# Differential attention: context units apart, and which engine scales which map

## The reference, cut to what matters

```python
def diff_attend(q, k, v, lam):
    s = jnp.einsum('bqhcd,bkhcd->bhcqk', q, k) * (q.shape[-1] ** -0.5)
    p = jax.nn.softmax(s.astype(jnp.float32), axis=-1)
    a = (p[:, :, 0] - lam * p[:, :, 1]).astype(v.dtype)
    return jnp.einsum('bhqk,bkhd->bqhd', a, v)
```

## Time and profile before

| what | value |
|---|---|
| median of 3 runs | 4229.64 us (4227.66 to 4230.34) |
| profiled execution | 4231.93 us, span 4230.1 us, clock 0.984 |
| busy, share of span | PE 94%, PE weight load 64%, DVE 40%, ACT 24%, POOL 19% |
| stage in layer 0 | from about 1886 to 1980 us of the span |
| stage in layer 1 | from about 3358 to 3431 us of the span |

### The profile page before, as it was taken

One profiled execution on the slowest core, in us unless ns is written; L12 is line 12 of the kernel. 1 busy time (PEld: TensorE's weight loads), 2 busy tenths in 40 slices (PEclk: granted clock), 3 DMA queues, 4 the chain that ended last, 5 costly groups with the idle time before them and its releaser, 6 DMA issues. The chain is left out here.

```text
span 4230.1 us, 65478 instructions
## 1 busy us (share of the span) xinstructions
PE 3996.5 (94%) x28448; PEld 2713.6 (64%) x28448; DVE 1671.5 (40%) x2600; ACT 1035.7 (24%) x2175; POOL 812.5 (19%) x640
## 2 busy tenths in 40 slices
PE   8999999999999999998999799999899999979888
PEld 6788889887888767566555443333576778833332
DVE  2585854374444342627434300000436464421102
ACT  2212521222111221516211321111314252221111
POOL 2100022113442021113233101000131234400000
PEclk9999999999999999999999899999999999989999
DMA  3584300122223212010112399999320102389997
GB/s 112 205 285 147 89 18 4 44 100 74 80 87 95 68 56 87 6 60 1 60 60 100 130 379 389 387 388 366 106 87 26 60 21 100 120 339 427 427 427 307
DMA packets 194195, 668.89 MB, mean 158 GB/s; under 512 B 11751, under 2 KB 75943, under 8 KB 169335
## 3 DMA queue, kind: packets, MB, share of 16 engines
q1 hardware_dynamic: 188022, 644.01, 40.3%
q0 software_dynamic: 5888, 20.70, 1.6%
HBM read 642.52 MB, written 22.15 MB: 157 GB/s over the span
## 5 line engine op out<-in xcount | busy, mean ns | idle before, releaser
L555 PE MATMUL psum<-arena 128*128 128x264 f32 (+2 forms) x7120 | 1781.8, 412 | 13.5 <-DVE arena L610 3.7
L555 PEld LDWEIGHTS psum<-arena 128*128 128x128 f32 x7120 | 1349.5, 190 | 439.5 <-issue 11.8
L1444 PE MATMUL psum<-arena 128*64 128x512 f32 x3072 | 697.6, 601 | 43.7 <-DMA arena<-in_w_e 39.3
L1444 PEld LDWEIGHTS psum<-arena 128*64 128x64 f32 x3072 | 211.9, 137 | 466.4 <-issue 425.4
L590 ACT ACTIVATE arena<-psum 128x256 f32<-128x256 f32 (+2 forms) x405 | 169.4, 418 | 925.9 <-PE psum L555 871.5
L454 POOL TENSOR_TENSOR arena<-arena 128x512 f32<-128x512 f32 (+1 forms) x114 | 160.1, 1405 | 1025.0 <-PE psum L555 964.8
L2406 DVE TENSOR_TENSOR arena<-arena,psum 128x512 f32<-128x512 f32 x32 | 22.0, 688 | 786.6 <-PE psum L1452 532.5
L382 PE MATMUL psum<-arena 128*128 128x265 f32 (+2 forms) x1120 | 256.1, 387 | 3.3 <-ACT arena L3110 3.3
L382 PEld LDWEIGHTS psum<-arena 128*128 128x128 f32 (+1 forms) x1120 | 208.9, 188 | 42.8 <-ACT arena L3110 3.7
L2860 PE MATMUL psum<-arena 64*64 64x64 f32 x7424 | 225.9, 220 | 8.4 <-issue 4.5
L2860 PEld LDWEIGHTS psum<-arena 64*64 64x64 f32 x7424 | 224.1, 135 | 11.4 <-issue 8.6
(11 more groups left out here) (415 smaller groups left out, 3967.6 us busy)
## 6 DMA issues: line engine op xcount, KB each, us to landing
arena<-in_w_e SPq DMA_DIRECT2D x192, 2048.0 KB, 12.3
arena<-in_w_in SPq DMA_DIRECT2D x38, 2048.0 KB, 8.0
arena<-in_w_ada SPq DMA_DIRECT2D x24, 2048.0 KB, 8.4
arena<-in_ffn_up SPq DMA_DIRECT2D x22, 1024.0 KB, 7.5
arena<-in_w_branch SPq DMA_DIRECT2D x6, 2048.0 KB, 7.8
arena<-in_ffn_down SPq DMA_DIRECT2D x8, 1408.0 KB, 7.9
arena<-in_w_in SPq DMA_DIRECT2D x16, 512.0 KB, 4.5
arena<-in_w_out SPq DMA_DIRECT2D x4, 2048.0 KB, 8.3
```

The costliest lines, as they stand in the source:

```text
L555: mm = pe.matmul(PS[:, bank, 0:cn], loaded, moved, start=fresh and k == 0, stop=k == h - 1, skip_group_check=not fresh)
L1444: mm = pe.matmul(PS[c * HD:c * HD + HD, b + (m > 0), :], x(kk), w[:, k, c * BW:c * BW + BW], start=(kk == 0), stop=(kk == KT - 1))
```

## The change

In layer 0 the order of a head's six units becomes context, full, full, context, full, full. Layer 1's list is the same as before.

In both layers POOL no longer scales map 1 by its inverse and the factor; it scales map 0 by its own inverse, with one scalar. DVE inverts the first sum alone (`first_inverse`), behind reduction 1 of the same unit. The second sum's inverse is taken in `normal`, multiplied there by the factor and by -1 in an instruction on one column, and used as the scalar of the combination, which is now map 1 times that scalar plus the scaled map 0. `normal` of unit n-1 stands between the two reductions of unit n.

```diff
         for h in range(DA_H):
-            da += [(h, True, q) for q in q_ctx] + [(h, False, CTX + n * P) for n in range(SEQ // P)]
+            full = [(h, False, CTX + n * P) for n in range(SEQ // P)]
+            half = len(full) // 2
+            da += [(h, True, q) for q in q_ctx[:1]] + full[:half] + [(h, True, q) for q in q_ctx[1:]] + full[half:]
...
             for n in range(len(da)):
-                x1 = at(DA_S(n, 1), DA_KEYS(n))
-                wt(pool, "da_r", n + 1)
-                inc(nc.gpsimd.tensor_scalar(x1, x1, at(cell(n, 2) + 1, 1), at(LAMC, 1), ALU.mult, ALU.mult), "da_x1")
+                x0 = at(DA_S(n, 0), DA_KEYS(n))
+                wt(pool, "da_r0", n + 1)
+                inc(nc.gpsimd.tensor_scalar(x0, x0, at(cell(n, 2), 1), None, ALU.mult), "da_x0")
...
-                def inverse(n):
-                    wt(dve, "da_e", 2 * n + 2)
-                    inc(V.reciprocal(at(cell(n, 2), 2), at(cell(n, 1), 2)), "da_r")
+                def first_inverse(n):
+                    wt(dve, "da_e", 2 * n + 1)
+                    inc(V.reciprocal(at(cell(n, 2), 1), at(cell(n, 1), 1)), "da_r0")
 
                 def normal(n):
                     x, x1 = (at(DA_S(n, m), DA_KEYS(n)) for m in range(2))
-                    wt(dve, "da_x1", n + 1)
-                    inc(V.scalar_tensor_tensor(out=x, in0=x, scalar=at(cell(n, 2), 1), in1=x1, op0=ALU.mult,
-                                               op1=ALU.subtract), "da_p")
+                    c = at(cell(n, 2) + 1, 1)
+                    wt(dve, "da_e", 2 * n + 2)
+                    step(V.reciprocal(c, at(cell(n, 1) + 1, 1)))
+                    step.done()
+                    step(V.tensor_scalar(c, c, at(LAMC, 1), -1.0, ALU.mult, ALU.mult))
+                    step.done()
+                    wt(dve, "da_x0", n + 1)
+                    inc(V.scalar_tensor_tensor(out=x, in0=x1, scalar=c, in1=x, op0=ALU.mult, op1=ALU.add), "da_p")
 
                 for n in range(len(da) + 1):
                     if n < len(da):
                         largest(n, 0)
                     if n:
-                        inverse(n - 1)
+                        normal(n - 1)
                     if n < len(da):
                         largest(n, 1)
-                    if n:
-                        normal(n - 1)
+                        first_inverse(n)
```

## The result

The changed kernel takes 4249.98 us (median of 5 runs, 4246.81 to 4254.74) against 4230.34 (5 runs, 4227.66 to 4234.47) for the kernel before: ratio 1.0047, interval 1.0034 to 1.0061, about 20 us slower (14 to 26). The forecast was 4240.4 with a range from 4232 to 4247. The direction was right, the size was not.

A forecast was written before the change was run, and what follows sets the result against it. The prediction took TensorE, busy nearly all the span, to bound the kernel, with waits in the two differential-attention stages. 7.1+2.6+0.7+0.4=+10.8 on the median 4229.64 gave 4240.4 us, range 4232 to 4247.

The forecast's parts named there:

- POOL's rate: POOL's one-scalar multiplication, both stages: 2.20 us on 768 elements, 0.93 on 256; rival that 0.98 holds: chance 0.10.
- The ring: Layer 1: combination, reduction 1, inverse and POOL follow one another, 4.30 us a unit against 3.81; +7.1.
- 14 turns: Layer 1: 14 unit steps of 4.30 us each, from unit 1's combination to unit 15's.
- Order, end and the clock at the start: Layer 0: unit order +2.6 us, later last combination +0.7, low clock at the stage's start +0.4.
- six triples: Layer 0: the three steps of half a head, 10.73 us against 10.50, counted six times.
- ScalarE's queue: Layer 0: copy waits behind the late second exponential, making a context step 3.2 us where 2.5 was possible.
- The clock's 0.4: Start of layer 0: a second full unit may partly pay the 1.2 GHz level, between 0 and 1.37 us.
- let what follows the stages run as before: Behind both stages: later work starts from their end, and nothing downstream takes the time back.
- TensorE could lose its clock again in the looser rings: Both stages: possible further loss beyond the slower case's 4245 us; times beyond 4247 had chance 0.05.

The follow-up runs named there:

- e1: Changed kernel with a second scalar, the immediate 1.0, and a second multiplication in POOL's scaling of map 0; 4236.93 us against 4232.21 for the kernel before.
- e2: Changed kernel with VectorE's reduction 1 of a unit ahead of the previous unit's combination, POOL's form kept; 4237.43 us against 4232.21 for the kernel before.
- e3: Changed kernel with layer 0's units in the old order (context, context, four full); 4249.02 us against 4232.21 for the kernel before.
- e5: Changed kernel with three unread TensorE products added near the end of each layer's stage; 4245.21 us against 4232.21 for the kernel before.
- e4: Kernel before with only the new unit order, plus a second scalar 1.0 in L1972's four POOL multiplications off the stage; 4231.46 us against 4231.82.
- e6: Kernel before with unread 512-column TensorE products added at the start of both stages; 4229.29 us against 4231.82.
- e8: Changed kernel with the edits of e1, e2, e5 and e6 together, new unit order kept; 4232.00 us against 4231.82 for the kernel before.

## Why the prediction was right and wrong

- **POOL's rate: right**, to 0.01 us at both sizes, from L1972's four records. The Trainium skill, "GPSIMD Engine Reference", section 4.1, has one-input work at about line rate: e1's form agrees (from 256 to 768 elements 0.428 us more, 0.84 ns an element), the changed kernel's does not (1.279 more, 2.50 ns).
- **The ring: right in mechanism**, shown from both sides by e1 and e2. Its term was 7.1 and measured 8.50. Of the 1.4 missing, 0.8 are 14 turns of 4.36 instead of 4.30; 0.6 are the clock at the stage's start: unit 1's scores took 2.93 where the kernel before has 2.33, its clock falling only within them. These 0.6 are not of the change's work in this stage: e3 and e5 have the same instructions in this stage up to there, with 2.31 and 2.35 and a stage of 71.86 and 71.90. e1 and e2 have 2.93. The three with 2.93 are the three that lost the clock behind layer 0; what would join the two, some 1340 us apart, no run here shows.
- **Layer 0: nearly right, in part by luck.** Order, end and the clock at the start were put at 3.7 and measured 4.26; six triples of 10.81 instead of 10.73 are the 0.5. ScalarE's queue did stand in the way, as worked out. The table splits the 4.26: the list alone 1.13 (e4), the new work of VectorE with POOL's fast form 1.60 more (e1), the slow form another 1.53. The clock's 0.4 was a choice between 0 and 1.37 that no row fixed; e1, e2 and e4 lost 0.45 or 0.46 there as well, but e5, with the same start, 1.32.
- **The failed step is the clock.** Its term counted the start of layer 0 alone (0.4), and the next sentence let what follows the stages run as before, from their end. Behind layer 0 it did not: +3.69, the largest part of the missing 5.65 (3.69, 0.6, 0.8 and 0.56, between 10.8 and the table's 16.45). The loss had been named, "TensorE could lose its clock again in the looser rings", and dismissed because full scores late in the stage kept 1.56. That row is from layer 1, with the rings as they were. The forecast's own steps put the last combination later and a context unit among the last units, so TensorE's waits there could have been counted, and the products behind them priced at the 1.2 GHz level: the earlier trace rows give its cost, 2.93 against 1.56. That would have made the loss a case with a price and a chance, not a certainty: e3 has like waits and keeps its clock.
- **Left open.** Between the 16.45 of the stages and the medians' 19.6 (14 to 26) nothing is placed; the stretch between the layers varies by as much. It matters: with all of the 5.65 the forecast would have been 4246, inside its range, and the rest of the way to 4249.98 is this unplaced part and the 0.7 by which the kernel before itself came out higher (4230.34 against 4229.64). Why e1 loses only part of the clock behind layer 0 and e2 all of it is not settled, nor why e3 keeps it: its TensorE waits there too (1.54 twice and 0.38 in its timeline), and the window from 1978 shows 1.00:

```profile
1978.00:1984.00 6.00, 4.08 (x35) 3.63 (x33) 3.94 (x7) 2.63 (x6) 2.20 (x1) 1.00 0.00 0
```

## What to carry to other kernels

Before an operand of an instruction is dropped as superfluous, look for the shorter form's own rows: here it was the slower one, and its four records were enough to forecast it. When a buffer or engine gets slower inside a short dependent stage, work out the ring and then also TensorE's waits at both ends of the stage, since the products behind a wait may run at half the clock. Unread products in those waits give that back, but they must cover every wait, since filling the first only moved the loss to the next (e6), and must be shorter than the wait, since longer ones delay what follows (e8).

## What the runs showed of the hardware

POOL's multiplication by one scalar per partition took 2.205 us on 128x768, with a second multiplication by the constant 1.0 0.908, and with a second scalar per partition 0.981; out of place, on 128x512, 1.562 and 0.689. Why the form with less arithmetic is the slow one, no run here shows.

At the end of layer 0 the granted clock fell after waits of no more than 1.28 and 1.54 us, with work of TensorE between and around them, and was still at 0.50 in the window that ends at 1988; in e5 the same stretch, with unread products in these waits, stood at 1.00. Where the clock falls varies between executions of the same instructions: at the start of layer 0 the first three full units' scores took 2.93, 1.75 and 1.82 in the changed kernel, and 1.67, 2.93 and 2.77 in e5.
